# Seven products per chunk: a running sum in one PSUM bank, its states copied out by ScalarE, three adds on VectorE

## The chip, the core and the metric

The kernel runs on one core of one Trainium2 chip. TensorE (PE) multiplies matrices into PSUM, VectorE (DVE), ScalarE (ACT) and GpSimd (POOL) do the elementwise work, and SyncE (SP) issues the loads of the weights. The metric is the device time of one launch in microseconds, as the median of three runs.

## What is computed

Two transformer blocks on one sequence of 512 tokens of width 1024. Most of the time goes into six feed-forward layers: two squared-ReLU MLPs of width 4096, and four SwiGLU layers of width 2816:

```python
h = _rmsnorm(x, norm_ffn[i]); x = x + _sq_relu_mlp(h, mlp_w_up[i], mlp_w_down[i])

def swiglu(x, w_gu, w_d):
    gate, up = jnp.split(x @ w_gu, 2, axis=-1)
    return (jax.nn.silu(gate) * up) @ w_d
```

Everything is float32. A product is made as three matmuls of rounded parts: high times high, high times low, low times high.

## The kernel before

**Tiling.** Tokens lie along the free axis, features across the 128 partitions. Weights arrive in chunks of 1 MB (`raw`, two slots). ACT makes the high part `whi` (L464 or L330), DVE the low part `wlo` (L336). The load of chunk n+2 waits until chunk n has its low part, because it reuses the slot (L320).

**Groups.** An FFN layer is cut into groups of 256 hidden columns: 16 in an MLP (`f0`, `f1`), 11 in a SwiGLU layer (`s00`, `s01`, `s10`, `s11`). A group has one chunk of `up` weights in an MLP (c = 0), two in a SwiGLU layer (gate is c = 0, up is c = 1), and one chunk for the down projection. `ffn_walk` makes each engine do `gu(g)` and then `down(g-1)`, so the elementwise work of one group has the down projection of the group before it as its cover. Groups alternate between the PSUM banks 0 to 3 and 4 to 7 (`half`).

**Seven products.** From group 4 of an MLP and group 3 of a SwiGLU layer on (`SEVEN`), the 2x2 block product of a chunk is made of seven block products and not eight, by sums of weight blocks and of token blocks. That is 24 MLP groups and 32 SwiGLU groups. The token sums are made once for a layer (`th`). The weight sums are made for each chunk: POOL forms them (`pool_weights`, L451 to L457, four operations), ACT takes their high part `x_hi` (L467), DVE their low part `x_lo` (L473). Each product has twelve matmuls of 256 columns (L508 to L510). The order is the table `PRODUCTS`; its last column is the bank:

- A in bank 0, B in bank 1, E in bank 2, C in bank 3;
- then A2 on top of A, E2 on top of E, C2 on top of C.

The four quarters of the result (left and right tokens of `tmp[0]` and `tmp[1]`, or of `tmp[2]` and `tmp[3]` for c = 1) are then put together by DVE and ACT. ACT copies A out of PSUM into `snap` (L621). DVE adds B to it (L735), adds E and then C to that (L744, L750), and adds what is in bank 2 after E2 and in bank 3 after C2 (L753). A2 is read from PSUM by the activation itself (L633), or multiplied with the gate for c = 1 (L775). PE writes E2 and C2 only when DVE has read E and C.

**Order around it.** The queues are in-order. ACT in a SwiGLU group: `whi` of the up chunk (L464, it waits for POOL's L457 and for PE to leave the slot), the copy of A (L621), `x_hi` (L467), the high part of the previous group's u (L660), the activations, `whi` of the down chunk (L330), the copy of the second A. DVE: the last adds of `down` (L855), the products gate x up of the previous group (L785, L788), `wlo` (L336), the adds of the seven products, `x_lo` (L473), the low parts of u (L794). In the MLPs the first ACT step of a group is `whi` of the down chunk (L330).

Of the kernel before, what the change touches and what calls it, by code (L numbers as in the profile page):

```python
# [41 lines left out]
def build(nc, a, out):  # L42
    ctx = ExitStack()
    with ctx:
# [246 lines left out]
        for n_ in ffn_base:  # L291
            f_ = FFN[n_]
            seven_base[n_], act7_base[n_], dve7_base[n_], scaled_base[n_] = n7, a7, d7, sc
            t_no[n_] = sum(m_ in SEVEN for m_ in t_no)
            k7 = sum(seven(n_, g_) for g_ in range(f_["groups"]))
            n7 += k7 * f_["gu"]
            a7 += k7 * (3 if f_["swiglu"] else 4)
            d7 += k7 * (8 if f_["swiglu"] else 3)
            sc += 2 * (f_["groups"] - k7) if f_["swiglu"] else 0
# [120 lines left out]
        def after_down(name, g):  # L420
# [5 lines left out]
        PRODUCTS = (("m", 0, 0, TB11, 0), ("x", XS2, 0, T2, 1), ("x", XS3, 0, T3, 2), ("m", 0, 1, T1, 3),  # L426
                    ("m", 4, 0, TB21, 0), ("m", 4, 1, T4, 2), ("x", XS4, 0, TB22, 3))
        P_A, P_B, P_E, P_C, P_A2, P_E2, P_C2 = range(7)
# [4 lines left out]
        def region(half, p):  # L433
            return pbank[half + PRODUCTS[p][4]][:, LEFT]

# [40 lines left out]
        def pe_seven(pe, name, g, c, n, half, free, i, dn):  # L476
# [3 lines left out]
            acts, dves = (3, 8) if f["swiglu"] else (4, 3)  # L480
            a0, d0 = act7_base[name] + acts * (g - SEVEN[name]), dve7_base[name] + dves * (g - SEVEN[name])
            pe.wait_ge(lo_ready, at(n + 1, i, dn))
            for p, (src, q, m, t, r) in enumerate(PRODUCTS):
                if p == P_B:
                    pe.wait_ge(xlo_ready, at(y + 1, i, k))
                if p <= P_C and c == 0:
                    free(p)
                elif p == P_A:
                    pe.wait_ge(seven_act, at(a0 + 2, i, 2 * acts))
                elif p == P_B:  # L490
                    pe.wait_ge(seven_dve, at(d0 + 1, i, 2 * dves))
                elif p in (P_E, P_C):
                    pe.wait_ge(gate_done, at(2 * (ffn_base[name] + g) + 1 + (p == P_C), i, 4))
                elif p == P_A2:
                    pe.wait_ge(seven_act, at(a0 + 2 * c + 1, i, 2 * acts))
                elif p == P_E2:
                    pe.wait_ge(seven_dve, at(d0 + 3 * c + 2, i, 2 * dves))
                elif p == P_C2:
                    pe.wait_ge(seven_dve, at(d0 + 3 * c + 3, i, 2 * dves))
                for j in range(4):  # L500
# [5 lines left out]
                    first = j == 0 and p <= P_C  # L506
                    last = j == 3
                    pe.matmul(pbank[half + r][:, LEFT], hi, th[:, j, t, 1, :], start=first, stop=False, skip_group_check=True)  # L508
                    pe.matmul(pbank[half + r][:, LEFT], hi, th[:, j, t, 0, :], start=False, stop=False, skip_group_check=True)  # L509
                    ins = pe.matmul(pbank[half + r][:, LEFT], lo, th[:, j, t, 1, :], start=False, stop=last, skip_group_check=True)  # L510
# [53 lines left out]
        def pe_ffn(pe, name, stage):  # L564
            f, b, bs = FFN[name], ffn_base[name], swi_base[name]

            def gu(g, n, i, dn, dt):
                half = 4 * (g % 2)
                for c in range(f["gu"]):
# [10 lines left out]
                    if seven(name, g):  # L580
                        if c == 0 and g == SEVEN[name]:
                            pe.wait_ge(t_lo, 4 * t_no[name] + 4)
                        pe_seven(pe, name, g, c, n + c, half, free, i, dn)
# [13 lines left out]
        def act_ffn(e, name):  # L597
# [8 lines left out]
            def gu_seven(g, n, i, dn, dt):  # L606
                half = 4 * (g % 2)
                acts = 3 if f["swiglu"] else 4
                a0 = act7_base[name] + acts * (g - SEVEN[name])
                if f["swiglu"]:  # L610
                    func = ACT.Silu
                else:
                    func = ACT.Relu

                def keep(c):
                    e.wait_ge(tiles_out, at(before[n + c] + P_A + 1, i, dt))
                    if c == 0:
                        e.wait_ge(gate_done, at(2 * (b + g - 1) + 2, i, 4))
                    else:
                        e.wait_ge(prod_done, at(2 * (bs + g - 1) + 2, i, 4))  # L620
                    e.activation(snap[:, c, :], region(half, P_A), ACT.Copy).then_inc(seven_act, 1)  # L621
                if f["swiglu"]:
                    act_weights(e, name, g, 1, n + 1, i, dn, dt, lambda: keep(0))
                    if deferred(name, g - 1):
                        swi_high(g - 1, i, dt)
                else:
                    keep(0)
                e.wait_ge(tiles_out, at(before[n] + P_A2 + 1, i, dt))
                if f["swiglu"]:
                    e.wait_ge(prod_done, at(2 * (bs + g - 1) + 2, i, 4))  # L630
                else:
                    e.wait_ge(uhi_done, at(2 * (b + g - 1) + 2, i, 4))
                e.activation(tmp[:, 0, LEFT], region(half, P_A2), func).then_inc(seven_act, 1)  # L633
                e.wait_ge(gate_done, at(2 * (b + g) + 1, i, 4))
                ins = e.activation(tmp[:, 1, :], tmp[:, 1, :], func)
                ins.then_inc(silu_done if f["swiglu"] else seven_act, 1)
                if f["swiglu"]:
                    act_hi(e, n + 2, i, dn, dt)
                    keep(1)
                e.wait_ge(gate_done, at(2 * (b + g) + 2, i, 4))  # L640
                ins = e.activation(tmp[:, 0, RIGHT], tmp[:, 0, RIGHT], func)
                ins.then_inc(silu_done if f["swiglu"] else seven_act, 1)
# [6 lines left out]
                for j in range(2):  # L649
                    u = 2 * (g % 2) + j  # L650
                    e.wait_ge(ulo_done, at(2 * (b + g - 1) + j + 1, i, 4))
                    e.wait_ge(seven_act, at(a0 + 4, i, 2 * acts))
# [63 lines left out]
        def dve_ffn(e, name, stage):  # L716
# [4 lines left out]
            def gu_seven(g, n, i, dn, dt):  # L721
                half = 4 * (g % 2)
                acts, dves = (3, 8) if f["swiglu"] else (4, 3)
                a0, d0 = act7_base[name] + acts * (g - SEVEN[name]), dve7_base[name] + dves * (g - SEVEN[name])

                def step(k):
                    e.wait_ge(seven_dve, at(d0 + k, i, 2 * dves))

                def part(c, p):
                    e.wait_ge(tiles_out, at(before[n + c] + p + 1, i, dt))  # L730
                    return region(half, p)

                def joined(c):
                    e.wait_ge(seven_act, at(a0 + 2 * c + 1, i, 2 * acts))
                    e.tensor_tensor(snap[:, c, :], part(c, P_B), snap[:, c, :], ALU.add).then_inc(seven_dve, 1)  # L735

                def last_quarter(c, meanwhile=None):
                    d = tmp[:, 2 * c + 1, RIGHT]
                    if c == 0 and not f["swiglu"]:
                        e.wait_ge(uhi_done, at(2 * (b + g - 1) + 2, i, 4))  # L740
                    src = part(c, P_E)
                    step(3 * c + 1)
                    third = tmp[:, 7, LEFT] if meanwhile else d
                    e.tensor_tensor(third, src, snap[:, c, :], ALU.add).then_inc(seven_dve, 1)  # L744
                    if meanwhile:
                        meanwhile()
                        e.wait_ge(ulo_done, at(2 * (b + g - 1) + 2, i, 4))
                    src = part(c, P_C)
                    step(3 * c + 2)
                    e.tensor_tensor(d, src, third, ALU.add).then_inc(seven_dve, 1)  # L750

                def outer(c, p, d, signal):
                    e.tensor_tensor(d, part(c, p), snap[:, c, :], ALU.add).then_inc(signal, 1)  # L753
                if f["swiglu"]:
                    if deferred(name, g - 1):
                        products(g - 1, i)
                    dve_lo(e, n + 1, i, dn, dt)
                joined(0)
                last_quarter(0)
                if f["swiglu"]:  # L760
# [2927 lines left out]
```

## Time and profile before

| | us |
|---|---|
| median of three runs | 3489.55 (3489.16 to 3490.47) |
| profiled execution | 3490.93 |
| its span, first to last instruction | 3489.2 |
| PE busy | 3408.1 (98%) |
| DVE / ACT / POOL busy | 2398.5 / 1466.2 / 1060.9 |

The page of the profile gives busy time by engine, the costliest groups of instructions with the idle time ahead of them and what ended it, and the chain that ended last. A matmul's recorded duration (280 ns for 256 columns) is longer than the distance from one matmul's start to the next, since they overlap. So starts are compared here, and not durations, where PE is read. Recorded ends are start plus duration.

### The profile page before, as it was taken

The page shows a single profiled execution, that of the slowest core. Times are in us where ns is not written, and L with a number is a line of the kernel's source. Part 1 is how long each engine was busy: PE and PEld are TensorE (multiplying, and loading weights), DVE is VectorE, ACT ScalarE, POOL GpSimd, SP SyncE. Part 2 cuts the span into 40 slices and gives each one's busy share as a digit, 9 for nine tenths or more (in the row PEclk, how much of TensorE's full clock was granted, in tenths as well). Part 3 has the DMA queues.
Part 4 walks back from the last instruction along what each step waited for, and adds up shares of the span by engine and source line. Part 5 has one row for each costly group of instructions (what it writes and reads, how often), then busy time and mean ns, then how long its engine had stood idle before and what let it go on. Part 6 is the DMA issues. An engine that isn't in the chain of part 4 may idle for free. (4 is left out here: it accounts for less than half of the span.)

```text
span 3489.2 us, 55972 instructions
## 1 busy us (share of the span) xinstructions
PE 3408.1 (98%) x21919; PEld 2865.7 (82%) x21919; DVE 2398.5 (69%) x3206; ACT 1466.2 (42%) x2080; POOL 1060.9 (30%) x687
## 2 busy tenths in 40 slices
PE   8999999999999999999999999999999999999998
PEld 6889988645889978997777789988998777778997
DVE  6687774465777777776577588878787434468786
ACT  5644442465444443333644343344334322244333
POOL 1243332010343235434023054524552100015452
PEclk9999999999999999999999999999999999999999
DMA  3332334100233223233100133222332222213331
GB/s 122 97 107 99 108 100 97 37 1 13 97 99 107 96 89 105 97 109 93 61 26 15 49 109 108 97 85 98 108 105 88 85 85 85 85 55 103 109 99 69
DMA packets 232578, 296.24 MB, mean 85 GB/s; under 512 B 21893, under 2 KB 201464, under 8 KB 232392
## 3 DMA queue, kind: packets, MB, share of 16 engines
q1 hardware_dynamic: 230864, 290.48, 25.7%
q0 software_dynamic: 1152, 3.05, 0.4%
q8 instruction: 130, 2.13, 0.3%
q14 instruction: 56, 0.46, 0.0%
q10 hardware_dynamic: 376, 0.12, 0.0%
HBM read 291.53 MB, written 2.10 MB: 84 GB/s over the span
## 5 line engine op out<-in xcount | busy, mean ns | idle before, releaser
L336 DVE TENSOR_TENSOR wlo<-raw,whi 128x2048 fp32r<-128x2048 f32 x266 | 662.1, 2489 | 277.4 <-ACT whi L330 248.1
L330 ACT ACTIVATE whi<-raw 128x2048 fp32r<-128x2048 f32 x178 | 340.8, 1914 | 647.7 <-PE bank L342 557.1
L340 PE MATMUL bank<-u_hi,whi 128*128 128x512 f32 x1440 | 563.0, 391 | 4.6 <-DVE arena L3485 2.4
L342 PE MATMUL bank<-u_hi,wlo 128*128 128x512 f32 x1440 | 560.8, 389 | 0.0
L341 PE MATMUL bank<-u_lo,whi 128*128 128x512 f32 x1440 | 560.2, 389 | 0.0
L340 PE MATMUL bank<-h_hi,whi 128*128 128x512 f32 (+1 forms) x1340 | 535.7, 400 | 21.5 <-DVE h_lo L1135 9.9
L342 PE MATMUL bank<-h_hi,wlo 128*128 128x512 f32 (+1 forms) x1340 | 522.2, 390 | 0.0
L341 PE MATMUL bank<-h_lo,whi 128*128 128x512 f32 (+1 forms) x1340 | 522.2, 390 | 0.0
L508 PE MATMUL bank<-th,whi 128*128 128x256 f32 x1408 | 394.7, 280 | 1.9 <-DVE tmp L744 1.9
L510 PE MATMUL bank<-th,wlo 128*128 128x256 f32 x1408 | 393.0, 279 | 0.0
L509 PE MATMUL bank<-th,whi 128*128 128x256 f32 x1408 | 392.9, 279 | 0.0
L464 ACT ACTIVATE whi<-raw 128x2048 fp32r<-128x2048 f32 x88 | 168.5, 1915 | 457.9 <-PE bank L342 213.5
L340 PEld LDWEIGHTS bank<-h_hi,whi 128*128 128x128 f32 x1340 | 253.2, 189 | 91.7 <-issue 31.3
L340 PEld LDWEIGHTS bank<-u_hi,whi 128*128 128x128 f32 x1440 | 270.3, 188 | 61.7 <-issue 4.3
L342 PEld LDWEIGHTS bank<-u_hi,wlo 128*128 128x128 f32 x1440 | 270.3, 188 | 57.7
L341 PEld LDWEIGHTS bank<-u_lo,whi 128*128 128x128 f32 x1440 | 270.4, 188 | 54.4 <-issue 0.2
L341 PEld LDWEIGHTS bank<-h_lo,whi 128*128 128x128 f32 x1340 | 253.5, 189 | 52.9 <-issue 3.6
L342 PEld LDWEIGHTS bank<-h_hi,wlo 128*128 128x128 f32 x1340 | 253.3, 189 | 52.8
L508 PE MATMUL bank<-th,x_hi 128*128 128x256 f32 x1056 | 296.1, 280 | 0.4
L510 PE MATMUL bank<-th,x_lo 128*128 128x256 f32 x1056 | 294.6, 279 | 0.0
L509 PE MATMUL bank<-th,x_hi 128*128 128x256 f32 x1056 | 294.6, 279 | 0.0
L508 PEld LDWEIGHTS bank<-th,whi 128*128 128x128 f32 x1408 | 264.3, 188 | 4.9 <-DVE tmp L744 2.7
(487 smaller groups left out, 6320.3 us busy)
## 6 DMA issues: line engine op xcount, KB each, us to landing
raw<-in_ffn_wgu SPq DMA_DIRECT2D x88, 1024.0 KB, 5.1
raw<-in_ffn_wd SPq DMA_DIRECT2D x44, 1024.0 KB, 4.9
raw<-in_mlp_w_up SPq DMA_DIRECT2D x32, 1024.0 KB, 5.3
raw<-in_mlp_w_down SPq DMA_DIRECT2D x32, 1024.0 KB, 4.8
raw<-in_odd_w_in SPq DMA_DIRECT2D x24, 1024.0 KB, 5.1
raw<-in_even_w_in SPq DMA_DIRECT2D x13, 1024.0 KB, 5.3
raw<-in_rg_w_in SPq DMA_DIRECT2D x8, 1024.0 KB, 5.6
raw<-in_odd_w_out SPq DMA_DIRECT2D x8, 1024.0 KB, 5.0
```

The source lines that it names most:

```text
L330: e.activation(whi[:, n % 2, :], raw[:, n % 2, :], ACT.Copy).then_inc(hi_ready, 1)
L336: e.tensor_tensor(wlo[:, n % 2, :], raw[:, n % 2, :], whi[:, n % 2, :].bitcast(F32), ALU.subtract).then_inc(lo_ready, 1)
L340: pe.matmul(o, w_hi, r_hi, start=first, stop=False)
L341: pe.matmul(o, w_hi, r_lo, start=False, stop=False)
L342: return pe.matmul(o, w_lo, r_hi, start=False, stop=last)
L464: e.activation(whi[:, n % 2, :], raw[:, n % 2, :], ACT.Copy).then_inc(hi_ready, 1)
L508: pe.matmul(pbank[half + r][:, LEFT], hi, th[:, j, t, 1, :], start=first, stop=False, skip_group_check=True)
L509: pe.matmul(pbank[half + r][:, LEFT], hi, th[:, j, t, 0, :], start=False, stop=False, skip_group_check=True)
L510: ins = pe.matmul(pbank[half + r][:, LEFT], lo, th[:, j, t, 1, :], start=False, stop=last, skip_group_check=True)
```

## The change

`PRODUCTS` gets a new order and new banks: R1, Q1, R2, A, R3, Q2, R4. The four R products (A, B, E and the product of E2 of before) accumulate in one bank, one on top of the other. Q1 and Q2 (C and C2 of before) share a second bank. A (A2 of before) has a third bank. For c = 1 the R bank is bank 3 and not bank 0, so that it can be written while the R bank of c = 0 is still to be read.

ACT copies the R bank after R1, R2 and R3 and the Q bank after Q1: three states go straight to the places of the outputs in `tmp`, and Q1 to `snap`. After R4 the bank holds a finished quarter, which is read by the activation (c = 0) or the multiplication (c = 1). DVE makes three adds for a chunk: A plus the state after R1; the state after R3 plus Q1, both in SBUF; Q2 plus the state after R2. PE writes R2 only after the copy of R1 (`kept` = 1), R3 after the copy of R2, R4 after the copy of R3, Q2 after the copy of Q1.

The copies for c = 0 write `tmp[0]` and `tmp[1]`, so the copy of R1 waits for both products gate x up of the previous group (`prod_done`), or for both squares in an MLP. The copies for c = 1 write `tmp[2]` and `tmp[3]` and wait for the low parts of u (`ulo_done`). On ACT the copy of the second R1 stands ahead of `whi` of the down chunk. On DVE `x_lo` of the up chunk stands ahead of the adds, and `products` makes its wide operation on `tmp[2]` and the narrow one on `tmp[3]`.

```diff
-        PRODUCTS = (("m", 0, 0, TB11, 0), ("x", XS2, 0, T2, 1), ("x", XS3, 0, T3, 2), ("m", 0, 1, T1, 3),
-                    ("m", 4, 0, TB21, 0), ("m", 4, 1, T4, 2), ("x", XS4, 0, TB22, 3))
+        PRODUCTS = (("m", 0, 0, TB11, 0), ("m", 0, 1, T1, 1), ("x", XS2, 0, T2, 0), ("m", 4, 0, TB21, 2),
+                    ("x", XS3, 0, T3, 0), ("x", XS4, 0, TB22, 1), ("m", 4, 1, T4, 0))
+        P_R1, P_Q1, P_R2, P_A, P_R3, P_Q2, P_R4 = range(7)
+        def region(half, c, p):
+            r = PRODUCTS[p][4]
+            return pbank[half + (3 if c and r == 0 else r)][:, LEFT]
...
             for p, (src, q, m, t, r) in enumerate(PRODUCTS):
-                if p == P_B:
+                if p == P_R2:
                     pe.wait_ge(xlo_ready, at(y + 1, i, k))
+                if p == P_R1:
+                    free(3 if c else 0)
+                elif p in (P_Q1, P_A) and c == 0:
+                    free(r)
+                elif p == P_Q1:
+                    pe.wait_ge(gate_done, at(2 * (ffn_base[name] + g) + 2, i, 4))
                 elif p == P_A:
                     pe.wait_ge(seven_dve, at(d0 + 1, i, 2 * dves))
+                else:
+                    kept = {P_R2: 1, P_Q2: 2, P_R3: 3, P_R4: 4}[p]
+                    pe.wait_ge(seven_act, at(a0 + 4 * c + kept, i, 2 * acts))
...
+                def first():
+                    if f["swiglu"]:
+                        e.wait_ge(prod_done, at(2 * (bs + g - 1) + 2, i, 4))
+                    else:
+                        e.wait_ge(uhi_done, at(2 * (b + g - 1) + 2, i, 4))
+                    keep(0, P_R1, tmp[:, 0, LEFT])
                 if f["swiglu"]:
+                    act_weights(e, name, g, 1, n + 1, i, dn, dt, first)
                 else:
+                    first()
+                keep(0, P_Q1, snap[:, 0, :])
+                keep(0, P_R2, tmp[:, 0, RIGHT])
+                if f["swiglu"] and deferred(name, g - 1):
+                    swi_high(g - 1, i, dt)
+                e.wait_ge(seven_dve, at(d0 + 1, i, 2 * dves))
+                rectify(tmp[:, 0, LEFT])
+                keep(0, P_R3, tmp[:, 1, RIGHT])
+                e.wait_ge(gate_done, at(2 * (b + g) + 1, i, 4))
+                rectify(tmp[:, 1, RIGHT])
+                e.wait_ge(gate_done, at(2 * (b + g) + 2, i, 4))
+                ins = rectify(tmp[:, 0, RIGHT])
...
+                ins = e.activation(tmp[:, 1, LEFT], made(0, P_R4), func)
                 if f["swiglu"]:
+                    e.wait_ge(ulo_done, at(2 * (b + g - 1) + 2, i, 4))
+                    keep(1, P_R1, tmp[:, 2, LEFT])
                     act_hi(e, n + 2, i, dn, dt)
+                    keep(1, P_Q1, snap[:, 1, :])
+                    keep(1, P_R2, tmp[:, 2, RIGHT])
+                    keep(1, P_R3, tmp[:, 3, RIGHT])
...
                 if f["swiglu"]:
+                    if late:
                         products(g - 1, i)
                     dve_lo(e, n + 1, i, dn, dt)
                     dve_weights_rest(e, name, g, 1, n + 1, i)
+                joined(0, P_A, 1, tmp[:, 0, LEFT], seven_dve)
+                if late:
+                    u_low(g - 1, i, (0,))
+                inner(0, gate_done)
+                if late:
+                    u_low(g - 1, i, (1,))
+                joined(0, P_Q2, 3, tmp[:, 0, RIGHT], gate_done)
                 if not f["swiglu"]:
                     return
                 dve_lo(e, n + 2, i, dn, dt)
+                joined(1, P_A, 1, tmp[:, 2, LEFT], seven_dve)
+                inner(1, seven_dve)
+                joined(1, P_Q2, 3, tmp[:, 2, RIGHT], seven_dve)
+                e.tensor_tensor(tmp[:, 3, LEFT], region(half, 1, P_R4), tmp[:, 1, LEFT], ALU.mult).then_inc(seven_dve, 1)
```

## Rows read from the trace of the kernel before

**Rows 1.** PE's waits over the whole span: engine line waited for: us, times, longest

```profile
PE bank L340 <- DVE h_lo L1135: 9.9, 12, 1.1
...
PE bank L508 <- DVE tmp L744: 1.9, 4, 0.6
```

**Rows 2.** Busy time (instructions) of PE, PEld, DVE, ACT, POOL: first SwiGLU layer

```profile
1333.00:1580.00 247.00, 246.49 (x1731) 230.80 (x1730) 194.82 (x227) 91.11 (x96) 106.94 (x58) 1.00 0.32 107
```

**Rows 3.** Timeline, undisturbed SwiGLU group: start us, us, engine line op, [idle <-releaser]

```profile
1396.13 0.28 PE L508 MATMUL bank<-th,whi 128*128 128x256 f32 x1
...
1404.61 0.28 PE L508 MATMUL bank<-th,x_hi 128*128 128x256 f32 x1
...
1404.81 0.42 DVE L753 TENSOR_TENSOR tmp<-bank,arena 128x256 f32<-128x256 f32 x1 [0.65 <-PE bank L510]
...
1426.84 0.28 PE L508 MATMUL bank<-th,whi 128*128 128x256 f32 x1
```

**Rows 4.** Timeline, first group of seven products of the first SwiGLU layer

```profile
1333.65 2.78 POOL L457 TENSOR_TENSOR sums_b<-raw,sums_b 128x512 f32<-128x512 f32 x1
1333.68 0.28 PE L508 MATMUL bank<-th,whi 128*128 128x256 f32 x1
...
1335.33 0.38 PE L508 MATMUL bank<-th,x_hi 128*128 128x256 f32 x1
...
1336.52 1.91 ACT L464 ACTIVATE whi<-raw 128x2048 fp32r<-128x2048 f32 x1 [5.50 <-POOL sums_b L457]
...
1338.34 0.37 ACT L621 ACTIVATE arena<-bank 128x256 f32<-128x256 f32 x1
...
1339.68 0.28 PE L508 MATMUL bank<-th,whi 128*128 128x256 f32 x1
...
1341.20 0.42 DVE L744 TENSOR_TENSOR tmp<-bank,arena 128x256 f32<-128x256 f32 x1
...
1341.68 0.38 PE L508 MATMUL bank<-th,whi 128*128 128x256 f32 x1 [0.43 <-DVE tmp L744]
...
1343.20 0.28 PE L508 MATMUL bank<-th,x_hi 128*128 128x256 f32 x1
```

**Rows 5.** ACT's waits over the whole span, one line

```profile
ACT whi L464 <- POOL sums_b L457: 22.0, 4, 5.5
```

**Rows 6.** Timeline, the same undisturbed SwiGLU group: ACT, DVE and POOL

```profile
1396.41 1.92 ACT L464 ACTIVATE whi<-raw 128x2048 fp32r<-128x2048 f32 x1 [7.62 <-PE bank L342]
...
1397.92 0.41 DVE L788 TENSOR_TENSOR tmp<-tmp 128x256 f32<-128x256 f32 x1
...
1398.23 0.36 ACT L621 ACTIVATE arena<-bank 128x256 f32<-128x256 f32 x1
...
1408.17 3.05 DVE L336 TENSOR_TENSOR wlo<-raw,whi 128x2048 fp32r<-128x2048 f32 x1 [0.25 <-ACT whi L330]
...
1416.59 1.31 POOL L451 TENSOR_TENSOR sums_b<-raw 128x512 f32<-128x512 f32 x1 [2.50 <-DMA raw<-in_ffn_wgu]
```

**Rows 7.** Timeline, undisturbed MLP group

```profile
447.22 0.28 PE L508 MATMUL bank<-th,whi 128*128 128x256 f32 x1
...
447.42 1.92 ACT L330 ACTIVATE whi<-raw 128x2048 fp32r<-128x2048 f32 x1 [4.78 <-PE bank L342]
...
449.24 0.36 ACT L621 ACTIVATE arena<-bank 128x256 f32<-128x256 f32 x1
```

**Rows 8.** Timeline, a SwiGLU group whose up chunk reached POOL late

```profile
3386.45 2.28 DVE L336 TENSOR_TENSOR wlo<-raw,whi 128x2048 fp32r<-128x2048 f32 x1
...
3391.33 2.69 POOL L457 TENSOR_TENSOR sums_b<-raw,sums_b 128x512 f32<-128x512 f32 x1
...
3395.08 0.28 PE L508 MATMUL bank<-th,whi 128*128 128x256 f32 x1
...
3396.58 0.41 DVE L788 TENSOR_TENSOR tmp<-tmp 128x256 f32<-128x256 f32 x1
```

**Rows 9.** Engines' busy time in a gap of PE: us, PE PEld DVE ACT POOL, clock

```profile
79.20:81.60 2.40, 0.53 (x3) 0.16 (x2) 2.40 (x3) 2.35 (x5) 2.40 (x2) 1.00 0.00 0
```

More of the change, by code:

```diff
@@ L505, in pe_seven @@
                         hi, lo = x_hi[:, s, q, j, :], x_lo[:, s, q, j, :]
-                    first = j == 0 and p <= P_C
+                    first = j == 0 and p in (P_R1, P_Q1, P_A)
                     last = j == 3
-                    pe.matmul(pbank[half + r][:, LEFT], hi, th[:, j, t, 1, :], start=first, stop=False, skip_group_check=True)
-                    pe.matmul(pbank[half + r][:, LEFT], hi, th[:, j, t, 0, :], start=False, stop=False, skip_group_check=True)
-                    ins = pe.matmul(pbank[half + r][:, LEFT], lo, th[:, j, t, 1, :], start=False, stop=last, skip_group_check=True)
+                    pe.matmul(out, hi, th[:, j, t, 1, :], start=first, stop=False, skip_group_check=True)
+                    pe.matmul(out, hi, th[:, j, t, 0, :], start=False, stop=False, skip_group_check=True)
+                    ins = pe.matmul(out, lo, th[:, j, t, 1, :], start=False, stop=last, skip_group_check=True)
                 ins.then_inc(tiles_out, 1)
@@ L607, in gu_seven, with made, keep @@
                 half = 4 * (g % 2)
-                acts = 3 if f["swiglu"] else 4
-                a0 = act7_base[name] + acts * (g - SEVEN[name])
+                func = ACT.Silu if f["swiglu"] else ACT.Relu
+                dves = 5 if f["swiglu"] else 1
+                d0 = dve7_base[name] + dves * (g - SEVEN[name])
+                def made(c, p):
+                    e.wait_ge(tiles_out, at(before[n + c] + p + 1, i, dt))
+                    return region(half, c, p)
+                def keep(c, p, d):
+                    e.activation(d, made(c, p), ACT.Copy).then_inc(seven_act, 1)
@@ L610, in gu_seven, with rectify @@
+                def rectify(d):
+                    return e.activation(d, d, func)
+                def first():
[4 more added lines that the diff above has]
+                    keep(0, P_R1, tmp[:, 0, LEFT])
                 if f["swiglu"]:
-                    func = ACT.Silu
+                    act_weights(e, name, g, 1, n + 1, i, dn, dt, first)
@@ L612, in gu_seven @@
                 else:
[L613 to L621, printed above, removed]
-                if f["swiglu"]:
[L623 to L635, printed above, removed]
+                    first()
@@ L737, in last_quarter @@
-                def last_quarter(c, meanwhile=None):
-                    d = tmp[:, 2 * c + 1, RIGHT]
[L739 to L750, printed above, removed]
@@ L752, in outer, with kept, joined @@
-                def outer(c, p, d, signal):
-                    e.tensor_tensor(d, part(c, p), snap[:, c, :], ALU.add).then_inc(signal, 1)
+                acts = 8 if f["swiglu"] else 5
+                a0 = act7_base[name] + acts * (g - SEVEN[name])
+                def kept(k):
+                    e.wait_ge(seven_act, at(a0 + k, i, 2 * acts))
+                def joined(c, p, k, d, signal):
+                    e.wait_ge(tiles_out, at(before[n + c] + p + 1, i, dt))
+                    kept(4 * c + k)
+                    e.tensor_tensor(d, region(half, c, p), d, ALU.add).then_inc(signal, 1)
```

73 lines of the change are left out of this document (16 added, 57 removed).

## The prediction

> **What bounds the kernel now.** I read PE first, since it is busy for 98% of the span. PE's waits [rows 1] say where it stands still: the longest entries are norms between the layers, which the change doesn't touch. Of the matmuls that it does touch only one line has a wait: L508 waits four times for DVE's L744, 1.9 us in all. The busy times [rows 2] say the same: in the seven-product groups of the first SwiGLU layer PE is busy for 246.49 of 247.00 us, with DVE at 194.82 and ACT at 91.11. So in these layers PE sets the time and all other engines are cover. A recorded matmul hides short gaps, though, so I compared starts. In an undisturbed SwiGLU group the first product starts at 1396.13, the seventh at 1404.61 and the next group at 1426.84 [rows 3]: 8.48 / 6 = 1.413 us, so about 1.415, for a product of twelve matmuls, and 30.71 us from group to group. There is nothing to win in such a group, and the change keeps 7 x 12 matmuls a chunk. It can only remove waits or add them.
>
> The waits of before are all in the first group of seven products of the four SwiGLU layers [rows 4]. I write T for a group's first matmul. There T is 1333.68; the second product should start at 1335.10 and starts at 1335.33, the sixth should start 1.415 after 1339.68 and starts at 1341.68. From these rows also comes what a late release costs: L744 ends at 1341.62, PE starts at 1341.68, and the next product comes at 1343.20, 1.52 later and not 1.415. So PE's schedule moves to the end of the releasing operation plus 0.16 us, and a release that ends more than 0.16 before a product is due costs nothing. The two waits together: 0.34 + 0.69, that is 1.03 us in this layer, and about 1.07 in each of the other three (same pattern): 4.3 us in all. This is the most that the change could win.
>
> **Part by part. DVE and ACT work.** In a SwiGLU group DVE has eleven short operations for the seven products and afterwards seven: -4 x 0.42 = -1.7 us. ACT has two copies and three activations, afterwards eight copies of 0.36 and four activations: some +2.3 us. In an MLP group -0.8 and +1.3. DVE isn't the bound, so its part is worth nothing by itself; ACT goes from 91.11 to some 110 of 247 us [rows 2], so its part costs nothing by itself either. What counts is the order.
>
> **The copy of R1, undisturbed group.** New is that PE's third product, R2, waits for ACT's copy of R1: it is due at T+2.83, so the copy has to end by T+2.67. ACT first makes `whi`, T+0.28 to T+2.20, and before it copied A at T+2.10 to T+2.46 [rows 6]. The new copy also waits for the second product gate x up, which ends at T+2.20 (1397.92 + 0.41) [rows 6]; a released ACT operation starts 0.03 later. So T+2.23 to T+2.59: in time by 0.08. Over the groups this DVE operation ends between T+1.8 and T+2.25, so the worst is in time by 0.03. In an MLP `whi` starts at T+0.20 and the copy at T+2.02 (449.24 against 447.22) [rows 7], it ends at T+2.38, and its new wait is for ACT's own squares, made long before: in time by 0.29. I take 0 for both, with an upper bound of 0.2 us for each of 28 SwiGLU groups (5.6 us), which is what a copy that starts 0.3 later would cost.
>
> **The other copies.** They follow their product: readers start 0.20 after the next product has started (1404.81 against 1404.61) [rows 3]. R2's copy is T+4.45 to 4.81, R3 is due at T+5.66. The add of A comes after `x_lo`, T+6.1 to 6.5, then the activation, then R3's copy at T+7.28 to 7.64, with R4 due at T+8.49. Each is in time by 0.69 after the 0.16. The second Q1 waits for `gate_done`, which comes at T+9.1 against T+11.3. Cost 0.
>
> **The down chunk's `whi`.** In the SwiGLU groups it is queued behind the copy of the second R1, so it starts at T+11.8 and not T+10.1. Behind it on ACT stand the copies of Q1 and R2 of the up chunk; Q1's copy moves to T+13.6, its user Q2 is due at T+17.0. DVE's `wlo` then starts at T+13.75 and not T+12.04 (1408.17) [rows 6]. PE needs it at T+19.8, so nothing is lost there. But this `wlo` also releases the load of the next up chunk, so POOL's work on that chunk, at T+20.46 before (1416.59) [rows 6], moves too. DVE and POOL wait for each other's whole instruction: DVE's L336 takes 3.05 when POOL is at work [rows 6] and 2.28 when it comes first, at T+22.08 of its group [rows 8], and POOL's last sum takes 2.69 behind DVE against 1.3 for a sum that waits for nobody. At T+9.4 to T+13.7 DVE makes no such operation now, so POOL's gate sums go through at 1.30 each, DVE gets its turn at about T+14.0, and `wlo` ends at T+16.2 and not T+15.1. POOL starts at about T+21.6. Taken in turn with DVE's 2.29 and 1.75, its last sum ends at T+30.4, 0.3 ahead of the next T; `whi` needs it at 0.28 behind T. A group that came late before shows this order [rows 8]: last sum 3391.33 + 2.69 = 3394.02, next T 3395.08, products done at 3396.58 + 0.41 = 3396.99, 1.91 behind T. It had no wait. If POOL comes after T+22.08, DVE's `wlo` goes first, the last sum ends at about 0.35 behind T and the copy of R1 ends at T+2.64: still in time, by 0.03. Cost 0, with the bound above.
>
> In these rows the queueing is by whole instructions. The Trainium skill, page "SBUF — State Buffer", section "SBUF: two separate sides", calls the pair of ports that DVE and POOL share an exclusive lock and says that whoever starts first has it for the whole instruction; with that the turn at T+22.08 is decided by who is first, as I have taken it.
>
> **The first group of a SwiGLU layer.** Here POOL is late: its last sum ends at 1336.43, `whi` runs 1336.52 to 1338.43, and the copy ran 1338.34 to 1338.71 [rows 4], that is T+4.66 to T+5.03. Before, its user was A2, the fifth product. Now it is R2, the third, due at T+2.83. R2 starts by T+5.03 + 0.16 = T+5.19: PE loses 2.36 us. `x_lo` of the gate chunk, which cost 0.34 before, is in time for R2. Later in the group: `x_lo` of the up chunk ends at T+8.8, the add of A at T+9.1, R3's copy at T+10.0, R4 due at T+10.85: nothing more is lost. Net 2.36 - 1.03 = +1.33 for this layer. All four layers have the same wait of ACT for POOL, 22.0 us in four times, the longest 5.5 [rows 5]; so the others have 2.37 - 1.07 = +1.30.
>
> **The last groups and the tail.** POOL is idle there, the last operation of c = 1 still follows the seventh product by 0.20, and the products after it are the same two. Cost 0. In an MLP ACT is done 0.45 earlier, with nothing behind it that PE waits for: 0.
>
> **The sum.** 1.33 + 3 x 1.30 = +5.2 us. The profiled execution has 3490.93, so 3496.1 for it; it stands 1.4 above the median of the runs. For the median: 3489.55 + 5.2 = 3494.8.
>
> **Rivals.** *A, slower: the copy of R1 is late in the undisturbed groups too.* Place: ACT's copy at T+2.2; it decides from the point at which the second product gate x up ends later than T+2.28 or `whi` starts later than T+0.48. For it: the margin is 0.03 to 0.08, and POOL's shift pushes both. Against it: in the late group the products were done at T+1.91. Price 0.1 to 0.2 in 28 groups, +2.8 to +5.6: 3497.6 to 3500.4. Chance 0.17.
>
> *B, slower: TensorE's clock falls behind the new gap of 2.4 us.* A gap of that size, 2.27 us, stands at 79.2, with clock 1.00 in it and behind it [rows 9], which speaks against. If the two products behind a gap ran at 1.2 GHz and not 2.4, each would take 1.4 longer: up to 2.8 in four layers, +11: 3506. Chance 0.04. [...]
>
> *C, the waits go away and none comes.* The x products start one place later and DVE has more time; if ACT's copy didn't hold R2 in the first groups, 4.3 us would be won: 3485.3. Against it: the copy stands behind `whi` in an in-order queue. Chance 0.05. *D, gain and loss even out*, for instance because POOL's last sum is done earlier in the first group (its 2.78 has 1.5 of waiting for `x_lo` in it): 3489 to 3492. Chance 0.06. The forecast itself keeps 0.68.
>
> **Range and chances.** 0.2% is 7.0 us and about what a measurement of this kernel can tell from no change. 3491.0 to 3500.5 takes in the forecast, most of A and part of D. Slower by over 0.2% is above 3496.5: B, most of A and a little of the forecast, 0.22. Faster by over 0.2% would need more than the 4.3 us that PE waits in all: 0.02. Within: 0.76.
>
> **What would show it.** PE waits for ACT before L508 in four places of about 2.4 us, at the third product of each layer's first group; all other groups keep 1.415 us a product, and the SwiGLU groups their 30.71 us. POOL's sums of the up chunk start about 1.1 later. DVE's busy time falls by some 70 us, ACT's rises by about 100. It is wrong if waits of 0.1 to 0.3 at L508 appear in most groups (A), if the clock of the SwiGLU layers is under 1.00 (B), or if the first groups lose less than 1 us (C).

## Result and profile after

The changed kernel takes 3501.54 us (median of eight runs, 3498.86 to 3505.21); the kernel before, beside it, 3490.29 (3489.16 to 3494.72). The ratio is 1.0031, with a 95% interval of 1.0022 to 1.0041: slower by 11 us, where the prediction had 5.

The page of after, profiled execution 3498.86 us; busy time, share of the span and instructions by engine:

```profile
span 3497.1 us, 55973 instructions
...
PE 3408.5 (97%) x21919; PEld 2867.4 (82%) x21919; DVE 2287.6 (65%) x3030; ACT 1576.5 (45%) x2400; POOL 1079.0 (31%) x687
```

PE's waits in after (engine line waited for: us, times, longest), to be laid beside [rows 1]:

```profile
PE bank L340 <- DVE h_lo L1123: 9.9, 12, 1.1
PE bank L507 <- ACT tmp L616: 8.9, 4, 2.2
```

The norm's wait is the same. The four waits of a product for DVE (1.9 us) are gone, and four waits for ACT's copy of R1 have come. The first SwiGLU layer's first group, timeline of after, which answers to [rows 4]; T is 1333.25:

```profile
1336.13 1.91 ACT L465 ACTIVATE whi<-raw 128x2048 fp32r<-128x2048 f32 x1 [5.51 <-POOL sums_b L458]
1337.94 0.37 ACT L616 ACTIVATE tmp<-bank 128x256 f32<-128x256 f32 x1
1338.07 2.29 DVE L336 TENSOR_TENSOR wlo<-raw,whi 128x2048 fp32r<-128x2048 f32 x1 [2.00 <-ACT whi L465]
...
1338.45 0.36 PE L507 MATMUL bank<-th,x_hi 128*128 128x256 f32 x1 [2.21 <-ACT tmp L616]
1338.65 0.28 PE L508 MATMUL bank<-th,x_hi 128*128 128x256 f32 x1
```

ACT stands 5.51 us for POOL, makes `whi` up to 1338.04, and only then copies R1, up to T+5.06. R2 starts at T+5.20. I take the time that a group loses from starts: from the start of its first matmul to the start of the last of its 168, less 19.67 us, which the same stretch takes without a wait. Here it is 2.45 us. A gap is given in the same way, from the start of the last matmul ahead of it to the start of the first one behind it: here 2.49 us, of which the profile calls 2.21 idle.

An undisturbed SwiGLU group of after, timeline (T is 1397.11); it answers to [rows 3] and [rows 6]:

```profile
1397.11 0.28 PE L507 MATMUL bank<-th,whi 128*128 128x256 f32 x1
...
1397.39 1.92 ACT L465 ACTIVATE whi<-raw 128x2048 fp32r<-128x2048 f32 x1 [7.62 <-PE bank L342]
...
1399.21 0.36 ACT L616 ACTIVATE tmp<-bank 128x256 f32<-128x256 f32 x1
...
1399.94 0.28 PE L507 MATMUL bank<-th,x_hi 128*128 128x256 f32 x1
...
1418.70 1.30 POOL L452 TENSOR_TENSOR sums_b<-raw 128x512 f32<-128x512 f32 x1 [4.26 <-DMA raw<-in_ffn_wgu]
...
1424.76 2.69 POOL L458 TENSOR_TENSOR sums_b<-raw,sums_b 128x512 f32<-128x512 f32 x1
...
1427.82 0.28 PE L507 MATMUL bank<-th,whi 128*128 128x256 f32 x1
```

The copy ends at T+2.46, R2 starts on time at T+2.83, and the next group comes 30.71 us later, as before. In none of the 28 such groups, nor in the 24 MLP groups, does PE lose time.

So far this is the prediction. What it lacks shows in the first groups of the four layers: busy time of PE, PEld, DVE, ACT, POOL in 23 us of each, then the granted clock, the DMA share and GB/s:

```profile
1333.00:1356.00 23.00, 20.79 (x173) 20.45 (x172) 12.28 (x14) 9.78 (x16) 10.07 (x6) 1.00 0.41 130
2081.00:2104.00 23.00, 20.79 (x163) 20.59 (x162) 11.79 (x12) 9.47 (x15) 7.98 (x5) 0.93 0.30 101
2438.00:2461.00 23.00, 20.76 (x173) 20.45 (x172) 13.68 (x14) 9.66 (x16) 10.21 (x6) 1.00 0.35 113
3216.00:3239.00 23.00, 20.78 (x173) 20.46 (x172) 12.26 (x14) 9.71 (x16) 10.15 (x6) 1.00 0.38 129
```

In the second layer the clock is 0.93 over the window. Matmuls behind the gap there, timeline:

```profile
2086.22 0.36 PE L507 MATMUL bank<-th,x_hi 128*128 128x256 f32 x1 [2.21 <-ACT tmp L616]
...
2088.53 0.41 PE L508 MATMUL bank<-th,whi 128*128 128x256 f32 x1
2088.74 0.41 PE L509 MATMUL bank<-th,wlo 128*128 128x256 f32 x1
2088.96 0.41 PE L507 MATMUL bank<-th,whi 128*128 128x256 f32 x1
```

They start 0.213 us apart and not 0.118: here the granted clock is at the lower of its two levels, 1.2 GHz and not 2.4, after the same wait of 2.21 us. This group lost 3.98 us by its starts, the three others 2.45 to 2.48.

### The profile page after: what moved, and what is told of

Read it like the earlier page. It is cut to its first block and busy times, and to the rows that moved or that the text cites. A ratio compares the mean times of both kernels' runs of the same rounds, so it can differ in the third digit from the quotient of the medians.

```text
span 3497.1 us, 55973 instructions
## 1 busy us (share of the span) xinstructions
PE 3408.5 (97%) x21919; PEld 2867.4 (82%) x21919; DVE 2287.6 (65%) x3030; ACT 1576.5 (45%) x2400; POOL 1079.0 (31%) x687
## 3 DMA queue, kind: packets, MB, share of 16 engines
q0 software_dynamic: 1152, 3.05, 0.4%
## 5 line engine op out<-in xcount | busy, mean ns | idle before, releaser
L336 DVE TENSOR_TENSOR wlo<-raw,whi 128x2048 fp32r<-128x2048 f32 x266 | 647.4, 2434 | 397.0 <-ACT whi L330 375.9
L340 PE MATMUL bank<-h_hi,whi 128*128 128x512 f32 (+1 forms) x1340 | 536.3, 400 | 21.6 <-DVE h_lo L1123 9.9
```

Source lines behind the costliest of these rows:

```text
L336: e.tensor_tensor(wlo[:, n % 2, :], raw[:, n % 2, :], whi[:, n % 2, :].bitcast(F32), ALU.subtract).then_inc(lo_ready, 1)
L340: pe.matmul(o, w_hi, r_hi, start=first, stop=False)
```

## Experiments

Theory Q (queue plus clock): all the loss is in the first groups, because the copy of R1 is queued behind `whi`, which waits for POOL; and on top of it the gap of 2.5 us brings the clock down in some of the layers, 1.5 us each time. Rival S: the loss is elsewhere, in small lateness spread over the undisturbed groups, in ACT's added work or in the shift of the down chunk's `whi`. Rival K: the clock falls because of the new order of products and copies, and not because of the gap.

There are three series of runs, each on one chip with its own runs of the kernel before: 3491.88 (27 runs), 3492.48 (33) and 3491.90 (26). Ratios are to the kernel before of the same series.

**The change again.** The unchanged second kernel, in the first and in the third series.

> The changed kernel once more, for its spread and for where TensorE's clock falls. Theory Q (in-order queue plus clock): the first group of each SwiGLU layer loses 2.4 us at the third product, waiting for ScalarE, which is 5.3 us more than before in all; on top of it the clock falls behind this gap in a changing number of the four layers, at 1.5 us each as in layer two of the profile. So 3496 to 3502 from run to run, median about 3501, and a profile in which the number of layers with a fall differs or falls in other layers. Rival S (the loss is elsewhere, in the undisturbed groups or the tail): the length of a run doesn't go with its mean clock.

> The changed kernel on the chip of these runs: 10 to 11 us over the kernel before, waits of 2.4 us at the third product of the four first groups, and the clock falling behind one to four of them.

Measured: 3502.1 (ratio 1.0035, 1.0021 to 1.0049) and 3500.99 (1.0026, 1.0016 to 1.0035). The first groups lost 1.79, 3.98, 3.97, 3.99 us in the one and 2.43, 3.99, 3.97, 3.98 in the other. Windows of the third profile, as above:

```profile
1333.00:1356.00 23.00, 20.81 (x173) 20.50 (x172) 12.23 (x14) 9.67 (x16) 10.18 (x6) 1.00 0.39 128
2078.00:2101.00 23.00, 20.78 (x161) 20.49 (x160) 11.89 (x12) 9.46 (x15) 8.52 (x6) 0.93 0.30 96
2436.00:2459.00 23.00, 20.76 (x161) 20.43 (x160) 12.03 (x13) 9.46 (x15) 10.60 (x6) 0.93 0.30 99
3216.00:3239.00 23.00, 20.79 (x162) 20.57 (x161) 11.60 (x13) 9.46 (x15) 8.10 (x6) 0.93 0.32 109
```

With the first profile the clock fell behind 7 of 12 gaps of the same length: one of four there, three of four in each of the other two.

**The queue undone, in the first groups alone.** `opening` puts ACT's copies of R1 and Q1 ahead of `whi` and the copy of R2 between `whi` and `x_hi`, and DVE's add of A ahead of `x_lo`:

```diff
+                if f["swiglu"] and g == SEVEN[name]:
+                    first()
+                    keep(0, P_Q1, snap[:, 0, :])
+                    act_weights(e, name, g, 1, n + 1, i, dn, dt, lambda: keep(0, P_R2, tmp[:, 0, RIGHT]))
+                    keep(0, P_R3, tmp[:, 1, RIGHT])
+                    e.wait_ge(seven_dve, at(d0 + 1, i, 2 * dves))
+                    rectify(tmp[:, 0, LEFT])
...
+                    if g == SEVEN[name]:
+                        joined(0, P_A, 1, tmp[:, 0, LEFT], seven_dve)
                     dve_weights_rest(e, name, g, 1, n + 1, i)
```

> Only the first group of each SwiGLU layer is put in another order: on ScalarE the copies of R1 and Q1 stand ahead of whi, that of R2 ahead of x_hi, that of R3 ahead of the first activation; on VectorE the add of A ahead of x_lo. Theory Q: R1's copy ends at T+2.0 and PE waits nowhere in that group, so the 4.3 us of waiting of the kernel before and the 9.5 us of the changed one are both gone and the clock stays up behind it: 3486.0. Rival S: what costs is not in that group, so 3492 or more stays.

> The reordered kernel once more, on the chip and in the call of its rivals: 6 us under the kernel before, and 16 under the changed one; its profile shows no clock fall in the seven-product groups of the SwiGLU layers.

Measured: 3485.53 (0.9982, 0.9973 to 0.9991), and in the second series 3487.49 (0.9986, 0.9977 to 0.9995). ACT in its first group, timeline (T is 1335.73):

```profile
1337.40 0.39 ACT L616 ACTIVATE tmp<-bank 128x256 f32<-128x256 f32 x1 [4.31 <-PE bank L509]
...
1338.76 0.39 ACT L616 ACTIVATE arena<-bank 128x256 f32<-128x256 f32 x1 [0.96 <-PE bank L509]
...
1339.04 1.91 ACT L465 ACTIVATE whi<-raw 128x2048 fp32r<-128x2048 f32 x1
...
1340.85 0.37 ACT L616 ACTIVATE tmp<-bank 128x256 f32<-128x256 f32 x1
1341.10 1.49 ACT L468 ACTIVATE x_hi<-sums_b 128x1536 fp32r<-128x1536 f32 x1
```

The copy now follows R1 at once (1337.40) and R2 needs it only at 1338.56. `whi` starts at T+3.3, 0.4 us later than in the changed kernel, and PE doesn't wait for it. PE has no wait in any first group, and only 0.41, 0.18 and 0.41 us in three second groups. This edit leaves every other part of the change in place, and the loss turns into a gain: so the slowdown is in the first groups, and the order of the products and ACT's added work cost nothing measurable. It is the fastest kernel here, 6.4 and 5.0 us under the kernel before (6 was expected of the second series), and no clock fell in these groups.

**Half of it.** In `r1_first` only the copy of R1 is put ahead of `whi`:

```diff
+                opening = f["swiglu"] and g == SEVEN[name]
+                if opening:
+                    first()
                 if f["swiglu"]:
-                    act_weights(e, name, g, 1, n + 1, i, dn, dt, first)
+                    act_weights(e, name, g, 1, n + 1, i, dn, dt, None if opening else first)
```

> As the changed kernel, but in the first group of each SwiGLU layer ScalarE makes the copy of R1 ahead of whi, and nothing else moves. Theory Q: the wait at the third product goes, the copy of R2 now ends at T+6.7 where R3 is due at T+5.66 (1.2 us lost), and R3's copy costs 0.4 more: 1.6 us a layer, 3490.3 - 4.3 + 6.3 = 3492.3. The gaps are short, so the clock doesn't fall behind them and the runs lie within 1 us of each other. Rival S: no change from 3501.

Measured: 3493.04 (1.0001, 0.9992 to 1.0010). Its waits of PE:

```profile
PE bank L507 <- ACT tmp L616: 3.8, 4, 1.0
```

The next copy in the queue, R2's, is now what ends last: 1.51 to 1.53 us a layer where 1.6 was expected, in two gaps of at most 1.2. No clock fell in these groups. Its runs lie 12 us apart (3487.31 to 3499.20) and not within 1: the clock falls in other stages too, on which more below.

**The gap alone, without the change.** `before_gap` is the kernel before with its old order and its DVE adds, but E also waits for the copy of A:

```diff
+                if p == P_E and c == 0 and f["swiglu"] and g == SEVEN[name]:
+                    pe.wait_ge(seven_act, at(a0 + 1, i, 2 * acts))
```

> The kernel before with one wait more: in the first group of each SwiGLU layer PE's third product waits for ScalarE's copy of the first, which it doesn't need. All the rest, banks, copies and adds, is as before. Theory Q: the products move to T+5.2 as in the changed kernel, 2.36 us lost a layer and the other waits of that group gone, so +5.3 us, and the clock falls behind the gap in some layers as often as in the changed kernel: 3496 to 3502, median near 3500. Rival K (the clock falls because of the new order of products and copies, not because of the gap): 3495.6, with the clock as in the kernel before. Rival S: 3490.

Measured: 3501.12 (1.0024, 1.0014 to 1.0033). Its wait and its windows of the four first groups:

```profile
PE bank L510 <- ACT arena L623: 7.1, 4, 1.8
...
1334.00:1357.00 23.00, 21.14 (x162) 20.62 (x161) 13.62 (x16) 7.07 (x8) 10.35 (x6) 0.93 0.37 129
2078.00:2101.00 23.00, 21.09 (x174) 20.52 (x173) 14.39 (x18) 7.14 (x9) 10.36 (x6) 1.00 0.42 139
2434.00:2457.00 23.00, 21.09 (x163) 20.61 (x162) 13.85 (x17) 7.07 (x8) 10.16 (x6) 0.93 0.38 127
3213.00:3236.00 23.00, 21.14 (x173) 20.61 (x172) 14.46 (x18) 7.07 (x8) 10.53 (x6) 1.00 0.40 137
```

The groups lost 3.92, 2.39, 3.93, 2.39 us, again 1.5 more where the clock is low. One added wait gives the old kernel the time of the new one. The order of products and copies is the old one here, so rivals S (3490) and K (3495.6, with no fall) are out.

**The same loss in two gaps.** `split_gap` is the changed kernel in which Q1 also waits for POOL's sums, so PE loses a part ahead of Q1 and the rest ahead of R2:

```diff
+                    if p == P_Q1 and f["swiglu"] and g == SEVEN[name]:
+                        pe.wait_ge(w_sum, 4 * y + 8)
```

> The changed kernel with one wait more in the first group of each SwiGLU layer: PE's second product (Q1) waits until GpSimd's last weight sum is done, at about T+2.75. PE still gets to the third product at T+5.2, held by ScalarE's copy as before, so the time lost in the queue is the same 2.4 us; but it stands still twice, for about 1.5 and 0.9 us, and not once for 2.4. Clock theory (the clock falls behind one long gap): no fall of the clock in these layers, 3491.9 + 5.5 = 3497.4 on the chip of the last runs, some 4.5 us under the changed kernel's 3502.1 there. Rival (the time over my sum is lost in something else than the clock, and goes with the change as a whole): same as the changed kernel, 3502.

Measured: 3493.58 (1.0002, 0.9993 to 1.0011). Two of its matmuls, and its windows:

```profile
1337.94 0.36 PE L509 MATMUL bank<-th,whi 128*128 128x256 f32 x1 [1.35 <-DVE fsum L845]
...
1340.21 0.36 PE L509 MATMUL bank<-th,x_hi 128*128 128x256 f32 x1 [0.62 <-ACT tmp L618]
...
1335.00:1358.00 23.00, 21.03 (x173) 20.53 (x172) 12.10 (x13) 10.03 (x16) 9.85 (x5) 1.00 0.39 133
2083.00:2106.00 23.00, 21.05 (x176) 20.45 (x175) 13.42 (x15) 10.04 (x16) 10.44 (x6) 1.00 0.35 118
2438.00:2461.00 23.00, 21.03 (x173) 20.52 (x172) 13.06 (x14) 9.47 (x15) 10.72 (x6) 1.00 0.39 126
3214.00:3237.00 23.00, 21.07 (x176) 20.46 (x175) 12.90 (x14) 10.51 (x16) 9.97 (x6) 1.00 0.39 132
```

(The first wait is for POOL's last sum; the profile names a DVE add that ended near it.) R2 starts no earlier after T than in the changed kernel, since the copy stands where it stood; the groups lost 2.45, 1.79, 2.45, 1.78 us. But the clock stays at 1.00 in all four, and the median is only 1.1 us over the kernel before, where the changed kernel's are 9.1 to 11.3 over it. Expected were 3497.4 if the long gap brings the clock down, and 3502 if the loss has another cause. The clock stayed up as the first says, but the median is 3.8 us under even that: the loss by starts is 8.5 us, against 11.4 to 14.4 in the changed kernel. On the rest more below.

**`whi` in halves.** In `whi_halves` the copy of R1 goes between two halves of `whi`:

```diff
+            if middle and g == SEVEN[name]:
+                e.activation(whi[:, n % 2, 0:CH // 2], raw[:, n % 2, 0:CH // 2], ACT.Copy)
                 middle()
+                e.activation(whi[:, n % 2, CH // 2:CH], raw[:, n % 2, CH // 2:CH], ACT.Copy).then_inc(hi_ready, 1)
```

> The changed kernel, but in the first group of each SwiGLU layer ScalarE makes whi of the up chunk in two halves with the copy of R1 between them. The copy ends 0.8 us earlier, about T+4.2, so PE loses 1.55 and not 2.4 us in one gap of about 1.7 us. Queue part: 4 x 0.8 = 3.2 us better than the changed kernel. Clock theory: the clock falls less often behind a gap of 1.7 us than behind 2.4, perhaps in none or one of the four layers, so 5 to 9 us better in all: 3493 to 3497 on the chip of the last runs. If the length of the gap doesn't matter to the clock, 3499.

Measured: 3494.11 (1.0001, 0.9992 to 1.0011); one gap of 1.61 to 1.65 and some 0.3 lost later, in all 1.85 to 1.89 a layer, and no clock fell in these groups.

**A longer gap.** In `gap_long` R2 of the first groups also waits for `x_hi` of the next chunk:

```diff
+                    if c == 0 and f["swiglu"] and g == SEVEN[name]:
+                        pe.wait_ge(xhi_ready, y + 2)
```

> The changed kernel with a longer gap: in the first group of each SwiGLU layer the third product also waits for x_hi of the up chunk, which it doesn't need (its end is at about T+6.15). PE loses 3.5 us and not 2.4, in one gap. If the clock's fall is a matter of the gap's length, it falls now in all four layers and costs 1.5 each, against one and three of four in the two profiles of the changed kernel: 4 x (3.5 - 2.4) = 4.4 us from the queue and some 3 from the clock, 7 over the changed kernel. If the falls have another cause than the gap: 4.4 over it.

Measured: 3509.85 (1.0046, 1.0032 to 1.0059). Its wait, and two of its four windows, which are alike:

```profile
PE bank L509 <- ACT x_hi L468: 14.2, 4, 3.6
...
1340.00:1363.00 23.00, 19.48 (x151) 19.23 (x150) 11.72 (x11) 9.19 (x15) 8.27 (x6) 0.93 0.28 92
2089.00:2112.00 23.00, 19.45 (x154) 19.27 (x152) 11.88 (x11) 9.37 (x15) 8.01 (x5) 0.93 0.27 93
```

The gap is 3.8 us, and the clock fell behind all four: 5.09 to 5.29 us lost. The median is 8.9 us over the changed kernel's of the same series, where 7 was expected with a fall in every layer and 4.4 if the falls have another cause than the gap.

**The shift of the down chunk's `whi`.** `opening_whi` is `opening` with that `whi` ahead of the copy of the second R1, in all groups, `opening_mix` only in the middle groups:

```diff
                 if f["swiglu"]:
+                    act_hi(e, n + 2, i, dn, dt)
                     e.wait_ge(ulo_done, at(2 * (b + g - 1) + 2, i, 4))
                     keep(1, P_R1, tmp[:, 2, LEFT])
-                    act_hi(e, n + 2, i, dn, dt)
```

> The kernel with the reordered first group, and besides in every SwiGLU group whi of the down chunk goes ahead of the copy of the second R1 on ScalarE (as in the kernel before). GpSimd's sums of the up chunk then start at T+20.5 again and not T+21.6. If the waits of 0.1 to 0.4 us at the third product that are left in the second group of three layers come from this shift, they go: 0.9 us better, 3484.6 where the reordered kernel had 3485.5. If the shift is harmless, as predicted, the two are equal within the noise. The copy of the second R1 ends at T+12.4, due at T+12.6: if it is late instead, each SwiGLU group loses 0.1 to 0.2 us and the kernel is 3 to 6 us slower than the reordered one.

> The reordered kernel, and whi of the down chunk ahead of the copy of the second R1 in all SwiGLU groups but the first and the last of the seven-product groups, where that order cost 0.5 and 0.05 us. PE's waits left in the reordered kernel (0.4, 0.2 and 0.4 us in the second groups of three layers) should go too: 1 us better in the trace, too little for the medians, so equal to the reordered kernel within 2 us.

Measured: 3489.92 (0.9993, 0.9984 to 1.0002) and 3488.86 (0.9990, 0.9981 to 0.9999). In `opening_whi` the waits of 0.4 in the second groups are gone, so they did come from the later `whi`; in their place the second R1's copy is late by 0.51 in each first group. In `opening_mix` the waits in the second groups did not go, against what was expected: 0.41, 0.20 and 0.22 us are left, since the first group ahead of them keeps the later `whi`. By starts `opening_mix` loses what `opening` loses and `opening_whi` 1.4 more. Neither beats `opening`; the medians, 2.4 and 1.4 us above its second one, don't separate the three.

**What a late copy costs in an MLP group.** `late_copy` is `opening` with two needless copies of 256 columns ahead of the copy of R1, in the MLP groups:

```diff
+                        for unused in (snap[:, 1, :], tmp[:, 7, LEFT]):
+                            e.activation(unused, rstd[:, LEFT], ACT.Copy)
                         first()
```

> A test of the rule that the prediction's margins rest on (a release that ends 0.16 us ahead of the product is free, later it costs the difference). Base is the reordered kernel; in each of the 24 MLP groups ScalarE makes two needless 256-column copies ahead of the copy of R1. Copies follow each other at 0.26 us, so R1's copy starts at T+2.54 and ends at T+2.90; the third product is due at T+2.83: 2.90 + 0.16 - 2.83 = 0.23 us lost in each group, 5.5 in all over the reordered kernel (3486 to 3487), thus about 3492. If the margin was not tight as I worked it out, nothing is lost.

Measured: 3499.05 (1.0017, 1.0008 to 1.0026). One such group, timeline:

```profile
409.56 0.40 ACT L639 ACTIVATE arena<-rstd 128x256 f32<-128x256 f32 x1
409.86 0.41 ACT L639 ACTIVATE tmp<-rstd 128x256 f32<-128x256 f32 x1
410.17 0.37 ACT L616 ACTIVATE tmp<-bank 128x256 f32<-128x256 f32 x1
...
410.59 0.39 PE L507 MATMUL bank<-th,x_hi 128*128 128x256 f32 x1
```

The copies start 0.30 and 0.31 apart where I had counted 0.26, so 18 of the 24 groups lost 0.33 and not 0.23 (the others 0.38 to 0.45). In this group PE starts 0.05 after the copy's end (410.54). It also bears out the margin of 0.29 [rows 7]: 0.61 of added work, less 0.29, is 0.32. The median is 7 us above the expected 3492, of which the larger loss (8.3 us in the MLP groups, not 5.5) explains 3; the profiled execution has 3495.78.

**All of it in one table.** PE's time lost in these groups, summed over a profile, against the medians (before loses 4.26 us):

| kernel | lost, us | more than before | medians, us more than before |
|---|---|---|---|
| `opening` | 0.4, 1.0 | -3.9, -3.3 | -6.4, -5.0 |
| `opening_mix` | 1.0 | -3.3 | -3.0 |
| `opening_whi` | 2.4 | -1.9 | -2.6 |
| `r1_first` | 6.1 | +1.8 | +1.2 |
| `whi_halves` | 7.5 | +3.3 | +1.6 |
| `split_gap` | 8.5 | +4.3 | +1.1 |
| `late_copy` | 9.5 | +5.3 | +7.2 |
| `before_gap` | 12.6 | +8.4 | +9.2 |
| changed kernel | 11.4, 13.7, 14.4 | +7.1, +9.5, +10.1 | +11.3, +10.2, +9.1 |
| `gap_long` | 20.7 | +16.4 | +18.0 |

(`opening`'s 0.4 is 1.0 less 0.63 from one group that ran faster, on which more below.) The loss by starts gives the medians to about 3 us, and to 4.2 for the changed kernel's first profile. Runs of one kernel scatter by more: the kernel before went from 3486.11 to 3496.75 in the third series, and its longer runs have a lower mean clock (3486.47 at 0.993, 3497.53 at 0.988, in the first).

The profiled executions show more, since there the loss and the time are of one and the same run. Span less the loss by starts is 3484.9 us for the kernel before, 3485.7, 3486.2 and 3484.1 for the changed kernel's three profiles, and 3485.8 for `split_gap`. So within an execution the loss by starts gives the changed kernel's time to 1.3 us. Over all fourteen profiles the rest goes from 3481.8 (`before_gap`) to 3490.3 (`opening_mix`), and it goes with the time that the clock spent at its lower level outside the first groups: 53 us in the one and 76 in the other, correlation 0.87. So the scatter is for the most part the clock in other stages.

## Why the prediction was too low

*What bounds the kernel, and where its waits are.* Right. PE sets the time, and the first groups were the only place.

*DVE and ACT work.* ACT rose by 110.3 us (about 100 predicted). DVE fell by 110.9, where 70 was predicted: the operations taken out come to 32 x 1.7 + 24 x 0.8 = 73.6. Most of the rest is shorter records of the same operations: the low parts of u went from 153.5 to 124.1 us and `wlo` from 662.1 to 647.4. I put that down to less waiting for POOL, as in the `wlo` of 3.05 and of 2.28 us of [rows 6] and [rows 8]; no run tests it. POOL rose by 18. None of it reached PE, as predicted.

*The undisturbed groups and rival A.* Right: the copy at T+2.10 to T+2.46, 0 us in 52 groups. Rival A is out.

*The shift of `whi` and POOL.* POOL's sums start at T+21.59 (21.6 predicted), and the last one ends 0.37 before the next T (0.3). The down chunk's `whi` is at T+11.9 (11.8). I took this for free; `opening` and `opening_whi` show that it costs 0.2 to 0.4 us in some second groups once the first groups are clean.

*The first groups, queue part.* Right: PE starts R2 at T+5.20 (5.19), and loses 2.45 to 2.48 without a fall of the clock (2.36). Most of the 0.1 more is in the restart, 0.22 us behind the copy's end and not 0.16 (see the last section). With 2.46 x 4 - 4.26 = 5.6 this is nearly the predicted 5.2. `opening` shows by experiment that the cause is the copy's place behind `whi`, and that rivals C and D, a gain, needed that place to be another.

*The clock, rival B.* This is the step that failed: the sum puts the clock at nothing. I gave its fall a chance of 0.04 on the evidence of one gap of 2.27 us with the clock at 1.00 behind it [rows 9]; from start to start as there, the new gap is 2.49. Those rows show the gap alone; here are windows that take in what follows it, the first of the kernel before, the second of `opening_mix`, where the same gap lies at 79.69 to 81.94:

```profile
81.60:85.00 3.40, 2.99 (x13) 2.16 (x14) 3.17 (x2) 1.19 (x2) 2.63 (x2) 1.00 0.00 0
...
80.00:92.00 12.00, 10.13 (x38) 8.19 (x38) 5.22 (x4) 8.00 (x13) 4.67 (x3) 0.86 0.00 0
```

The clock stayed up in the one trace that I had, and fell behind this very gap in three of the fourteen profiles (`opening_mix`, `whi_halves`, `gap_long`). Behind the gaps of the first groups it fell in 7 of 12 layers of the changed kernel (2.46 to 2.52 us) and in 2 of 4 of `before_gap` (2.02 to 2.07); one instance could not tell never from about every second time. The price was mis-sized as well, in the other direction: 1.5 us for a fall and not up to 2.8. That two products would run at the lower clock stands on no row; in the second layer of the first profile a fall slows one product to 2.52 us and the next to 1.83, instead of 1.41 each. So 7 / 3 = 2.3 falls x 1.52 = 3.5 us, and 5.6 + 3.5 = 9.1 against the 11.3, 10.2 and 9.1 of the medians. With chance 0.6 a layer, the step should have added 3.6 us to the likeliest case, and the range's top should have held four falls, 4 x 1.52 = 6.1 above 3494.8. Even this top, 3500.9, is just under the measured 3501.54; the kernel before, beside it, was 0.7 above the value that the prediction starts from.

The Trainium skill, page "TensorE: Matmul & The Clock Gate", section "What's actually happening", says that the point at which the clock changes depends on where in a free-running window the first matmul lands. That equal gaps here are sometimes followed by a fall and sometimes not fits it, but no run here tests it.

*What stays open.* Which of several equal gaps is followed by a fall. The last 0 to 2 us of the changed kernel's 9 to 11 in the medians, like `split_gap`'s being 3 under its sum, are within the scatter from the clock's falls in other stages; in the profiled executions the loss by starts gives both to 1.3 us.

## What to carry to other kernels

Before an operation is given a new reader, look at what stands ahead of it in its in-order queue in the first iteration too, not only in the steady one: here the copy that 52 groups got for nothing had 5.5 us of POOL's lateness in front of it in four. Price a gap of TensorE by its length and by the clock behind it, and count how often the clock falls over several gaps and several executions before calling it safe. Where a wait can't be avoided, split it: here two gaps of 1.6 and 0.9 us brought no fall in four layers, and one of 2.5 brought seven in twelve.

## What the hardware showed that was not expected

**The clock behind short gaps.** In the first groups there was no fall behind gaps of at most 1.2 to 1.65 us (0 of 12 layers in `r1_first`, `split_gap` and `whi_halves`), 9 of 16 behind 2.0 to 2.5 us, 4 of 4 behind 3.8. The nine falls began 0 to 1.5 us after the matmuls went on, and each cost about 1.5 us. These counts are from groups that are dense otherwise; in the norms and token mixers the clock fell behind other patterns as well.

**A faster rhythm.** Matmuls of 256 columns normally start 0.118 us apart. In a few groups they start 0.113 apart, in most of these from a wait to the end of the group, with no clock recorded above 1.00. The first layer of the changed kernel's second profile, timeline, each line one matmul in three:

```profile
1339.61 0.35 PE L507 MATMUL bank<-th,x_hi 128*128 128x256 f32 x1 [2.19 <-ACT tmp L616]
...
1340.03 0.28 PE L507 MATMUL bank<-th,x_hi 128*128 128x256 f32 x1
...
1340.37 0.28 PE L507 MATMUL bank<-th,x_hi 128*128 128x256 f32 x1
...
1340.71 0.28 PE L507 MATMUL bank<-th,x_hi 128*128 128x256 f32 x1
```

Three matmuls take 0.34 us and not 0.353, and the group lost 1.79 us and not 2.45. `split_gap` has it in two layers, the kernel before and `whi_halves` for one or two products. `opening` has it in one group from the third product on, with no wait ahead of it, so a wait is not what it takes. What sets it off is open.

**The restart.** It comes in two sizes. In the kernel before, `r1_first` and `before_gap` the first matmul behind a wait starts 0.05 us after its releaser's end, and the second follows it by 0.22 and not 0.118. Together this is the 0.16 that the prediction took from [rows 4]. Behind the wait for R1's copy in the changed kernel, and in `whi_halves` and `opening_whi`, it starts 0.14 after the end (1338.31 to 1338.45 in the first timeline above) and the second follows by 0.20: together 0.22. What decides between the two is open.
